# The border of mixing stage and feed in a single-core encoder step: the sample's columns of T1 and T2, the weights of three products, T1's parts and the second product change place

## The chip, the cores and the metric

One core of a Trainium2 chip (trn2) runs the whole step as one program. The time is the device time of one execution in microseconds; lower is better. The engines are TensorE (PE), VectorE (DVE), ScalarE (ACT), GpSimd (POOL) and SyncE (SP), the last used here only to issue DMAs.

## The reference, cut to what matters

One layer of an encoder for 1024 prompt rows and 64 sample rows of width 1024, in float32. The change lies where the first of these lines ends and the feed begins; projection and attention ahead of them are not touched.

```python
hp = xp + mixed @ w_out                      # mixing stage, 1024 prompt rows
xp = hp + _swiglu(hp, norm_ffn_g, w_gate, w_up, w_down)   # the feed
hs = xs + mixed_s @ w_out                    # the same for 64 sample rows
xs = hs + _swiglu(hs, norm_ffn_g, w_gate, w_up, w_down)

def _swiglu(h, g, w_gate, w_up, w_down):
    n = _rms_norm(h, g)
    return (silu(n @ w_gate) * (n @ w_up)) @ w_down
```

## The kernel before, in words

**Numbers in two parts.** Every matrix product is made of three: each float32 operand is split into a high part (a cast to the engine's reduced form, by ACT) and a low part (operand minus high part, by DVE or POOL), and PE adds high*high, high*low and low*high.

**The feed's products.** `n @ w_gate` and `n @ w_up` are made with seven products instead of eight (a Strassen-Winograd scheme): n, transposed, has four blocks B11, B21, B12, B22 (`raw_n[0][0]`, `raw_n[1][0]`, `raw_n[0][1]`, `raw_n[1][1]`), each 128 partitions by 4 groups by 544 rows of n. The first index is the half of the 1024 features, the second the half of the 1088 rows. The sample's 64 rows are the last 64 columns (480 to 543) of B12 and B22. Four sums are needed: T1 = B12 - B11 (written over B11), T2 = B22 - T1 (in `spare`), T3 = B22 - B12 (over B12), T4 = B21 - T2 (over B21). Product 0 takes B11, 1 B21, 2 T2, 3 T1, 4 T3, 5 T4, 6 B22. The parts of operand k lie in `part_hi[k]` and `part_lo[k]`. A product of a unit u is 24 matmuls: two column halves of 272, four feature groups, three part pairs (L2799 to L2801 in `feed`, L2056 to L2058 where it is made in the mixing stage). There are 22 units (11 pairs of 128 columns of each of gate and up).

**The weights' side.** Of each 256 columns of a weight the blocks a11, a12, a21, a22 and four sums (`s1`, `s2`, one in place, `s4`; `w_sum_dve`, L2579) are the stationary operands. ACT casts each one's high part into a ring of six slots (L2036, L2466), POOL writes the low part (L2042, L2430). Slot 0 of the first unit lies in an unused corner of `mT_hi`, slots 1 and 2 in `shared` where w_out's low half lay (free once the last mixing product is done).

**The mixing stage** (`mix`) goes through nine row tiles, in the order 0, 4, 1, 5, 2, 6, 3, 7 and last the sample's (index 8, 64 rows). Per tile: PE multiplies by w_out (two halves), DVE adds the residual (L1872, L1870), ACT takes the squares (L1833), POOL the root (L66, L68), DVE the norm (`xn`, L1877), PE turns `xn` (`turn_n`, L1967), ACT copies the result into `raw_n` (L1843). After each pair of tiles 128 more columns of all four blocks are there ("chunk"; the first has 96, since the second half of the rows begins at row 544), and ACT and DVE make the parts of B11 and B21 (L1812, L1885), T1 and T2 (L1894, L1896), T2's parts (L1818, L1911), and T3 and T4 (L1904, L1905) of it. After the last chunk's B11 parts PE makes the first product at the stage's end (`first_product_pe`), ahead of the sample's `turn_n`.

**The border.** `mix` and `feed` are two blocks: no engine begins the second before all have ended the first. Within a block each engine has its own queue in program order, and semaphores say what it waits for: `n_hi` and `n_lo` count high and low parts of n, `sums` the T's, `w_sums`, `w_hi_done`, `w_lo_done` the weights', `multiplied` finished products.

**The feed's first unit.** DVE begins with T1, T2 of the sample's columns, T2's low part of them (L2544, L2548, L2563), T3 of them (L2552), all of T1's low part (544 columns times 4 = 2176 elements), one weight sum (L2579), T4 of them (L2556), then the sums of products 0 to 2 from PSUM (L2596, L2600), T3's low part (L2563), and so on. ACT begins with T2's high part, the weight of product 2, T1's high part (L2474) and the weight of product 3. PE begins with product 1, SP loads the next unit's weights once T4 is done (L2012).

## Time and profile before

| | us |
|---|---|
| median of 3 runs | 1459.32 (1458.92 to 1460.43) |
| the profiled execution, its own time | 1457.65 |
| its span, first to last instruction | 1455.9 |
| PE busy | 1390.5 (96%) |
| DVE busy | 1023.3 (70%) |
| ACT busy | 627.0 (43%) |
| POOL busy | 391.7 (27%) |
| mixing stage ends, feed begins (in the span) | about 748 |
| mean granted TensorE clock | 0.985 of full |

Times of rows are microseconds from the span's start. An engine's busy time is that of its instructions; a matmul counts until its modelled end, so two in a row overlap. The profile names the idle time before an instruction in square brackets with what ended it; "issue" is a wait for nothing that the profile shows, "PEq" is the sequencer of PE, which is how the border of two blocks appears.

### The profile page before, as it was taken

What the parts mean: (1) busy time and instruction counts of PE and PEld (TensorE: products, weight loads), DVE (VectorE), ACT (ScalarE), POOL (GpSimd) and SP (SyncE); (2) the same over time, 40 slices, a digit from 0 to 9 for tenths busy, and PEclk for the clock granted to TensorE, in tenths of its full rate; (3) what the DMA queues carried; (4) which work ended last, traced back from release to release, by engine and by line L of the source; (5) the groups of instructions that cost most, each with busy time, mean ns of one, the idle gap of its engine ahead of it and who ended that gap; (6) DMA issues with size and microseconds to landing.
All of it is one profiled execution on the core that took longest, in us unless ns stands there. A gap on an engine that the chain in (4) does not pass through costs nothing. (4 is left out here: it accounts for less than half of the span.)

```text
span 1455.9 us, 23782 instructions
## 1 busy us (share of the span) xinstructions
PE 1390.5 (96%) x9152; PEld 1197.5 (82%) x9152; DVE 1023.3 (70%) x1378; ACT 627.0 (43%) x1154; POOL 391.7 (27%) x319
## 2 busy tenths in 40 slices
PE   7999999789999999999979999999999999999998
PEld 5778888667777766678869999999999998788886
DVE  6886868598876878955688666676666667654466
ACT  7524333268887776623253232222223223543343
POOL 2100000100010000011136454455445445654344
PEclk9999999889999999999999999999999999999999
DMA  7232320364443555453313444443344447954454
GB/s 253 74 136 95 116 76 33 129 187 119 125 104 105 145 144 163 120 167 122 105 54 136 147 140 161 147 169 132 119 145 162 146 154 237 346 176 159 160 181 174
DMA packets 176936, 209.66 MB, mean 144 GB/s; under 512 B 19456, under 2 KB 118136, under 8 KB 175416
## 3 DMA queue, kind: packets, MB, share of 16 engines
q1 hardware_dynamic: 171992, 197.32, 42.0%
q10 hardware_dynamic: 4832, 10.82, 2.0%
q8 instruction: 74, 1.21, 0.3%
q14 instruction: 38, 0.31, 0.1%
HBM read 148.78 MB, written 59.31 MB: 143 GB/s over the span
## 5 line engine op out<-in xcount | busy, mean ns | idle before, releaser
L1613 PE MATMUL ps_aT<-ident,z 128*128 128x128 f32 (+1 forms) x568 | 96.5, 286 | 2.1 <-DVE z L1447 2.1
L1269 ACT COPY aT<-ps_aT 128x512 f32<-128x512 f32 (+2 forms) x168 | 86.6, 523 | 26.1 <-PE ps_aT L1613 25.4
L683 PE MATMUL ps_proj<-shared 128*128 128x512 f32 x224 | 90.1, 402 | 4.6 <-DVE shared L540 3.0
L685 PE MATMUL ps_proj<-shared 128*128 128x512 f32 x224 | 88.3, 394 | 0.0
L684 PE MATMUL ps_proj<-shared 128*128 128x512 f32 x224 | 88.3, 394 | 0.0
L2480 ACT COPY aux<-ps_feed 128x544 f32<-128x544 f32 x22 | 13.5, 612 | 170.1 <-PE ps_feed L2801 170.1
L2430 POOL TENSOR_TENSOR ring_more<-staging,ring_more 128x512 fp32r<-128x512 f32 x45 | 69.4, 1547 | 56.5 <-ACT ring_more L2466 56.4
L1613 PEld LDWEIGHTS ps_aT<-ident,z 128*128 128x128 f32 (+1 forms) x568 | 63.8, 142 | 24.8 <-issue 14.7
L2430 POOL TENSOR_TENSOR shared<-staging,shared 128x512 fp32r<-128x512 f32 x41 | 60.0, 1468 | 86.0 <-ACT shared L2466 86.0
L1447 DVE TENSOR_TENSOR_SCAN z<-z,near 128x1024 f32<-128x1024 f32 (+7 forms) x64 | 82.7, 1337 | 0.0
L2694 DVE TENSOR_TENSOR blocks<-ps_feed,blocks 128x512 f32<-128x512 f32 x56 | 35.9, 681 | 66.0 <-PE ps_feed L2830 66.0
L2799 PE MATMUL ps_feed<-shared,ring_more 128*128 128x272 f32 x264 | 76.6, 290 | 1.8 <-issue 1.8
L2799 PE MATMUL ps_feed<-parts_early,shared 128*128 128x272 f32 x256 | 74.5, 291 | 2.1 <-PEq L1691 2.1
L2801 PE MATMUL ps_feed<-shared,ring_more 128*128 128x272 f32 x264 | 76.2, 289 | 0.0
L2800 PE MATMUL ps_feed<-shared 128*128 128x272 f32 x264 | 76.1, 288 | 0.0
L2800 PE MATMUL ps_feed<-parts_early,ring_more 128*128 128x272 f32 x264 | 76.1, 288 | 0.0
L2801 PE MATMUL ps_feed<-shared 128*128 128x272 f32 x264 | 76.1, 288 | 0.0
L2800 PE MATMUL ps_feed<-shared,ring_more 128*128 128x272 f32 x264 | 76.1, 288 | 0.0
L2801 PE MATMUL ps_feed<-parts_early,ring_more 128*128 128x272 f32 x264 | 76.0, 288 | 0.0
L2799 PE MATMUL ps_feed<-parts_early,ring_more 128*128 128x272 f32 x264 | 76.0, 288 | 0.0
L2799 PE MATMUL ps_feed<-shared 128*128 128x272 f32 x264 | 75.6, 286 | 0.0
L2800 PE MATMUL ps_feed<-parts_early,shared 128*128 128x272 f32 x256 | 74.5, 291 | 0.0
(351 smaller groups left out, 4520.4 us busy)
## 6 DMA issues: line engine op xcount, KB each, us to landing
staging<-s_dram SPq DMA_DIRECT2D x50, 256.0 KB, 3.6
staging<-in_w_gate SPq DMA_DIRECT2D x11, 1024.0 KB, 7.8
blocks<-in_w_up SPq DMA_DIRECT2D x11, 1024.0 KB, 5.4
blocks<-in_w_down SPq DMA_DIRECT2D x11, 1024.0 KB, 9.8
t_dram<-blocks SPq DMA_DIRECT2D x11, 1024.0 KB, 3.9
s_dram<-blocks SPq DMA_DIRECT2D x11, 1024.0 KB, 5.2
w_raw<-in_w_in SPq DMA_DIRECT2D x10, 1024.0 KB, 5.3
staging<-t_dram SPq DMA_DIRECT2D x30, 256.0 KB, 4.1
```

Source lines behind the costliest of these rows:

```text
L683: nc.tensor.matmul(res, a_hi[:, k, cols], b_hi[:, k], start=start, stop=False)
L684: nc.tensor.matmul(res, a_hi[:, k, cols], b_lo[:, k], start=False, stop=False)
L685: return nc.tensor.matmul(res, a_lo[:, k, cols], b_hi[:, k], start=False, stop=(k == HK - 1))
L1269: last = nc.scalar.copy(aT[:, G % AT, 0:f], ps_aT[:, G % 2, 0:f])
L1447: nc.vector.tensor_tensor_scan(back, back, mask[:, ::-1], 1.0, ALU.mult, ALU.max).then_inc(ready, 1)
L1613: last = nc.tensor.transpose(ps_aT[0:m, G % 2, k], z(x, at, m), t["ident"][:, :])
L2430: nc.gpsimd.tensor_tensor(w_lo, product_source(m)[0], w_hi.bitcast(F32), ALU.subtract).then_inc(w_lo_done, 1)
L2480: nc.scalar.copy(two(first), bank(u, 0)).then_inc(first_done, 1)
L2694: nc.vector.tensor_tensor(place, ps, place, ALU.add).then_inc(corners[name], 1)
L2799: nc.tensor.matmul(res, w_hi[:, k], x_hi, start=(k == 0), stop=False)
L2800: nc.tensor.matmul(res, w_hi[:, k], x_lo, start=False, stop=False)
L2801: last = nc.tensor.matmul(res, w_lo[:, k], x_hi, start=False, stop=(k == HK - 1))
```

## The change

- **Mixing stage, PE:** `first_product_pe` takes the number of the product. Product 0 is made where it was; after the sample's `turn_n` product 1 follows, out of the feed.
- **Weights:** ACT casts the blocks of products 1 and 2 after the last mixing product (before: 1), POOL corrects both ahead of the sample's `row_norm` (before: 1 after it); both leave the feed.
- **T1 and T2 of the sample's columns** and T2's parts of them are made at the end of the mixing stage, as a fifth chunk (480 to 543).
- **T1's parts:** columns 0 to 479 in the mixing stage (ACT ahead of the sample's copies, DVE after T2's low part of the fourth chunk), 480 to 543 as the feed's first work.
- **T3 and T4 of the fourth chunk** (352 to 479) leave the mixing stage and are made in the feed together with the sample's columns (192 columns times 4 = 768 elements each), ahead of the weight sum.
- The counts that waits ask for are shifted accordingly. No DMA is added or removed.

```diff
@@ -1747,6 +1747,13 @@
         NC = len(chunks)
+        chunks.append((ends[-1], TH))
+        def t2_made(c):
+            return 4 * c + 2 if c < NC else 4 * NC
         block = ctx.enter_context(nc.Block())
@@ -1786,10 +1793,13 @@
             for i in range(NT + 1):
+                if i == NT:
+                    w_low_pool(nc, pool, t, 1)
+                    w_low_pool(nc, pool, t, 2)
                 if i >= 1:
                     row_norm(i - 1)
-                if i >= NT - 1:
-                    w_low_pool(nc, pool, t, i - NT + 1)
+                if i == NT - 1:
+                    w_low_pool(nc, pool, t, 0)
                 if i + 2 < NT:
@@ -1814,7 +1824,7 @@
                 a, b = chunks[c]
-                act.wait_ge(sums, 4 * c + 2)
+                act.wait_ge(sums, t2_made(c))
                 nc.scalar.copy(part_hi[2][:, :, a:b], t["spare"][:, :, a:b]).then_inc(n_hi, 1)
@@ -1825,6 +1835,7 @@
                     w_high_act(nc, act, t, 1)
+                    w_high_act(nc, act, t, 2)
                 if i >= 1:
@@ -1837,6 +1848,10 @@
                         w_high_act(nc, act, t, 0)
+                    if i == NT:
+                        high_sum(NC - 1)
+                        nc.scalar.copy(part_hi[3][:, :, 0:ends[-1]], raw_n[0][0][:, :, 0:ends[-1]]).then_inc(n_hi, 1)
                     for j in range(2):
@@ -1844,8 +1859,9 @@
                     high_first(i // 2 - 1)
-                if i >= 3 and i % 2 == 1:
+                if i >= 3 and i % 2 == 1 and i < NT:
                     high_sum(i // 2 - 1)
+            high_sum(NC)
@@ -1889,25 +1905,25 @@
                 b11, b12, b22 = raw_n[0][0][:, :, a:b], raw_n[0][1][:, :, a:b], raw_n[1][1][:, :, a:b]
-                dve.wait_ge(n_out, 4 * (c + 1))
-                dve.wait_ge(n_lo, 3 * c + 1)
+                dve.wait_ge(n_out, min(4 * (c + 1), 2 * NT))
+                dve.wait_ge(n_lo, 3 * min(c, NC - 1) + 1)
                 nc.vector.tensor_tensor(b11, b12, b11, ALU.subtract).then_inc(sums, 1)
-                dve.wait_ge(sums, 4 * c + 1)
+                dve.wait_ge(sums, t2_made(c) - 1)
                 nc.vector.tensor_tensor(t["spare"][:, :, a:b], b22, b11, ALU.subtract).then_inc(sums, 1)
 ...
                 b12, b21, b22 = raw_n[0][1][:, :, a:b], raw_n[1][0][:, :, a:b], raw_n[1][1][:, :, a:b]
-                dve.wait_ge(sums, 4 * c + 2)
-                dve.wait_ge(n_lo, 3 * c + 2)
+                dve.wait_ge(sums, t2_made(c))
+                dve.wait_ge(n_lo, 3 * min(c, NC - 1) + 2)
                 nc.vector.tensor_tensor(b12, b22, b12, ALU.subtract).then_inc(sums, 1)
 ...
                 a, b = chunks[c]
-                dve.wait_ge(n_hi, 3 * c + 3)
+                dve.wait_ge(n_hi, 3 * c + 3 if c < NC else 3 * NC + 2)
                 nc.vector.tensor_tensor(part_lo[2][:, :, a:b], t["spare"][:, :, a:b],
@@ -1941,8 +1957,12 @@
                     w_sum_dve(nc, dve, t, 1)
-            second_sums(NC - 1)
             low_sum(NC - 1)
+            dve.wait_ge(n_hi, 3 * NC + 1)
+            nc.vector.tensor_tensor(part_lo[3][:, :, 0:ends[-1]], raw_n[0][0][:, :, 0:ends[-1]],
+                                    part_hi[3][:, :, 0:ends[-1]].bitcast(F32), ALU.subtract).then_inc(n_lo, 1)
+            first_sums(NC)
+            low_sum(NC)
@@ -2000,8 +2020,11 @@
             pe.wait_ge(m_lo, 2 * NT)
-            first_product_pe(nc, pe, t, 3 * NC - 2)
+            first_product_pe(nc, pe, t, 0, 3 * NC - 2)
             turn_n(NT - 1)
+            pe.wait_ge(h_added, 2 * (NT - 1))
+            first_product_pe(nc, pe, t, 1, 3 * NC - 1)
@@ -2017,6 +2040,10 @@
     return x[:, 0:HK, 0:P], x[:, HK:, 0:P], x[:, 0:HK, P:], x[:, HK:, P:]
+def first_factor(t, m):
+    return t["s2"] if m == 2 else first_blocks(t)[m]
@@ -2033,26 +2060,28 @@
     act.wait_ge(t["pair_loaded"][0], 16)
-    nc.scalar.copy(t["ring_first"][m][0], first_blocks(t)[m]).then_inc(t["w_hi_done"], 1)
+    if m == 2:
+        act.wait_ge(t["w_sums"], 2)
+    nc.scalar.copy(t["ring_first"][m][0], first_factor(t, m)).then_inc(t["w_hi_done"], 1)
 ...
     w_hi, w_lo = t["ring_first"][m]
-    nc.gpsimd.tensor_tensor(w_lo, first_blocks(t)[m], w_hi.bitcast(F32), ALU.subtract).then_inc(t["w_lo_done"], 1)
-def first_product_pe(nc, pe, t, parts_done):
-    pe.wait_ge(t["w_lo_done"], 1)
+    nc.gpsimd.tensor_tensor(w_lo, first_factor(t, m), w_hi.bitcast(F32), ALU.subtract).then_inc(t["w_lo_done"], 1)
+def first_product_pe(nc, pe, t, m, parts_done):
+    pe.wait_ge(t["w_lo_done"], m + 1)
     pe.wait_ge(t["n_lo"], parts_done)
-    w_hi, w_lo = t["ring_first"][0]
+    w_hi, w_lo = t["ring_first"][m]
     HK, CW = w_hi.shape[1], t["half"] // 2
 ...
         cols = slice(c * CW, (c + 1) * CW)
-        res = t["ps"][:, 0, c, 0:CW]
+        res = t["ps"][:, m, c, 0:CW]
         for k in range(HK):
-            x_hi, x_lo = t["part_hi"][0][:, k, cols], t["part_lo"][0][:, k, cols]
+            x_hi, x_lo = t["part_hi"][m][:, k, cols], t["part_lo"][m][:, k, cols]
             nc.tensor.matmul(res, w_hi[:, k], x_hi, start=(k == 0), stop=False)
@@ -2286,11 +2315,7 @@
-            return 3 * (NT // 2) + max(0, k - 1)
-        def sums_done(k):
-            return 4 * (NT // 2) + k
+            return 3 * (NT // 2) + 2 + max(0, k - 2)
@@ -2298,7 +2323,7 @@
                     sp.wait_ge(n_lo, parts_done(2))
-                    sp.wait_ge(sums, sums_done(4))
+                    sp.wait_ge(sums, 4 * (NT // 2) + 2)
                 elif u >= 2:
@@ -2424,7 +2449,7 @@
         def _(pool):
-            for m in range(2, M):
+            for m in range(3, M):
                 pool.wait_ge(w_hi_done, m + 1)
@@ -2467,10 +2492,10 @@
-                src = (spare, raw_n[0][0], raw_n[0][1], raw_n[1][0], raw_n[1][1])[k - 2]
-                cols = slice(near if k == 2 else 0, TH)
-                if k < 6:
-                    act.wait_ge(sums, sums_done((2, 1, 3, 4)[k - 2]))
+                src = (raw_n[0][0], raw_n[0][1], raw_n[1][0], raw_n[1][1])[k - 3]
+                cols = slice(near if k == 3 else 0, TH)
+                if k in (4, 5):
+                    act.wait_ge(sums, 4 * (NT // 2) + k - 3)
                 nc.scalar.copy(part_hi[k][:, :, cols], src[:, :, cols]).then_inc(n_hi, 1)
@@ -2509,8 +2534,6 @@
-            split_n(2)
-            split_w(2)
             split_n(3)
@@ -2535,31 +2558,19 @@
         def _(dve):
-            def sum_n(k):
-                rest = slice(near, TH)
-                b11, b12, b21, b22 = raw_n[0][0], raw_n[0][1], raw_n[1][0], raw_n[1][1]
-                if k == 0:
-                    dve.wait_ge(n_lo, parts_done(1))
-                    nc.vector.tensor_tensor(b11[:, :, rest], b12[:, :, rest], b11[:, :, rest],
-                                            ALU.subtract).then_inc(sums, 1)
-                elif k == 1:
-                    dve.wait_ge(sums, sums_done(1))
-                    nc.vector.tensor_tensor(spare[:, :, rest], b22[:, :, rest], b11[:, :, rest],
-                                            ALU.subtract).then_inc(sums, 1)
-                elif k == 2:
-                    dve.wait_ge(sums, sums_done(1))
-                    nc.vector.tensor_tensor(b12[:, :, rest], b22[:, :, rest], b12[:, :, rest],
-                                            ALU.subtract).then_inc(sums, 1)
-                else:
-                    dve.wait_ge(sums, sums_done(2))
-                    nc.vector.tensor_tensor(b21[:, :, rest], b21[:, :, rest], spare[:, :, rest],
-                                            ALU.subtract).then_inc(sums, 1)
+            def sum_n():
+                rest = slice(near - P, TH)
+                b12, b21, b22 = (x[:, :, rest] for x in (raw_n[0][1], raw_n[1][0], raw_n[1][1]))
+                dve.wait_ge(sums, 4 * (NT // 2))
+                dve.wait_ge(n_lo, parts_done(2))
+                nc.vector.tensor_tensor(b12, b22, b12, ALU.subtract).then_inc(sums, 1)
+                nc.vector.tensor_tensor(b21, b21, spare[:, :, rest], ALU.subtract).then_inc(sums, 1)
             def split_n(k):
-                src = (spare, raw_n[0][0], raw_n[0][1], raw_n[1][0], raw_n[1][1])[k - 2]
-                cols = slice(near if k == 2 else 0, TH)
+                src = (raw_n[0][0], raw_n[0][1], raw_n[1][0], raw_n[1][1])[k - 3]
                 dve.wait_ge(n_hi, parts_done(k))
+                cols = slice(near if k == 3 else 0, TH)
                 nc.vector.tensor_tensor(part_lo[k][:, :, cols], src[:, :, cols], part_hi[k][:, :, cols].bitcast(F32),
@@ -2712,13 +2723,9 @@
-            sum_n(0)
-            sum_n(1)
-            split_n(2)
-            sum_n(2)
             split_n(3)
+            sum_n()
             sum_w(0, 2)
-            sum_n(3)
             for u in range(NU):
@@ -2847,7 +2854,7 @@
             for u in range(NU):
-                for s in range(0 if u else 1, NPROD):
+                for s in range(0 if u else 2, NPROD):
                     product(u, s)
@@ -2962,9 +2969,9 @@
-            at = 6 * WIDTH + 2 * HK * P
-            t["ring_first"] = [None, [shared[:, at + a * HK * P:at + (a + 1) * HK * P]
-                                      .rearrange("p (k n) -> p k n", k=HK) for a in range(2)]]
+            at = 6 * WIDTH
+            t["ring_first"] = [None] + [[shared[:, at + (2 * m + a) * HK * P:at + (2 * m + a + 1) * HK * P]
+                                         .rearrange("p (k n) -> p k n", k=HK) for a in range(2)] for m in (1, 2)]
             mix(nc, t)
```

## Rows read from the trace of the kernel before

**Rows 1.** Windows by stage: length, busy us of PE, PEld, DVE, ACT, POOL (instructions), clock, DMA.
```profile
741.00:756.50 15.50, 9.03 (x58) 8.67 (x57) 11.59 (x15) 8.35 (x12) 6.30 (x5) 0.78 0.08 18
756.50:776.00 19.50, 16.30 (x126) 15.73 (x125) 18.45 (x16) 7.80 (x10) 14.00 (x7) 1.00 0.50 162
776.00:1206.00 430.00, 430.00 (x3432) 430.00 (x3431) 283.25 (x314) 119.57 (x182) 210.24 (x146) 1.00 0.42 145
```

**Rows 2.** Timeline of PE, 738 to 770: start, us, line, out<-in [idle before <-releaser].
```profile
738.02 0.29 PE L2056 MATMUL ps_feed<-parts_early,mT_hi 128*128 128x272 f32 x1
...
740.91 0.29 PE L2058 MATMUL ps_feed<-parts_early,mT_hi 128*128 128x272 f32 x1
...
745.55 0.78 PE L1967 MATMUL ps_feed<-ident,xn 64*128 64x64 f32 x8 [4.35 <-DVE xn L1877]
...
748.45 0.56 PE L2799 MATMUL ps_feed<-parts_early,shared 128*128 128x272 f32 x1 [2.12 <-PEq L1691]
...
752.67 0.38 PE L2799 MATMUL ps_feed<-parts_early,shared 128*128 128x272 f32 x1
...
760.67 0.36 PE L2799 MATMUL ps_feed<-shared,ring_more 128*128 128x272 f32 x1 [0.96 <-issue]
...
769.40 0.36 PE L2799 MATMUL ps_feed<-part_late,shared 128*128 128x272 f32 x1 [1.45 <-issue]
```

**Rows 3.** Timeline of DVE, 718 to 761.
```profile
718.37 1.28 DVE L1877 SCALAR_TENSOR_TENSOR xn<-h_ring,rstd,g 128x1024 f32<-128x1024 f32 x1 [1.47 <-POOL rstd L68]
...
736.40 1.82 DVE L1885 TENSOR_TENSOR parts_early<-blocks,parts_early 128x768 fp32r<-128x768 f32 x2
...
741.74 0.69 DVE L1896 TENSOR_TENSOR blocks<-blocks 128x512 f32<-128x512 f32 x1
...
743.22 2.28 DVE L1877 SCALAR_TENSOR_TENSOR xn<-h_ring,rstd,g 64x1024 f32<-64x1024 f32 x1 [0.79 <-POOL rstd L68]
...
747.29 0.69 DVE L1911 TENSOR_TENSOR parts_early<-blocks,parts_early 128x512 fp32r<-128x512 f32 x1 [0.59 <-ACT parts_early L1818]
...
748.30 0.42 DVE L2544 TENSOR_TENSOR blocks<-blocks 128x256 f32<-128x256 f32 x1 [0.32 <-PEq L1691]
...
749.66 0.43 DVE L2563 TENSOR_TENSOR parts_early<-blocks,parts_early 128x256 fp32r<-128x256 f32 x1 [0.47 <-ACT parts_early L2474]
...
752.09 2.43 DVE L2563 TENSOR_TENSOR shared<-blocks,shared 128x2176 fp32r<-128x2176 f32 x1 [1.67 <-ACT shared L2474]
...
754.43 1.78 DVE L2579 TENSOR_TENSOR staging<-staging 128x512 f32<-128x512 f32 x1
...
757.73 2.85 DVE L2563 TENSOR_TENSOR shared<-blocks,shared 128x2176 fp32r<-128x2176 f32 x1
```

**Rows 4.** Timeline of ACT, 738 to 752.
```profile
738.22 0.62 ACT L2036 CAST shared<-staging 128x512 fp32r<-128x512 f32 x1 [1.45 <-PE ps_feed L1990]
...
746.05 0.69 ACT L1843 COPY blocks<-ps_feed 128x256 f32<-128x256 f32 x2 [3.76 <-PE ps_feed L1967]
...
749.22 0.40 ACT L2474 CAST parts_early<-blocks 128x256 fp32r<-128x256 f32 x1 [1.97 <-DVE blocks L2548]
...
750.05 2.00 ACT L2474 CAST shared<-blocks 128x2176 fp32r<-128x2176 f32 x1
```

**Rows 5.** Timeline of POOL, 743 to 756.
```profile
743.16 1.26 POOL L2042 TENSOR_TENSOR shared<-staging,shared 128x512 fp32r<-128x512 f32 x1
...
752.65 3.01 POOL L2430 TENSOR_TENSOR ring_more<-staging,ring_more 128x512 fp32r<-128x512 f32 x1 [1.08 <-ACT ring_more L2466]
```

**Rows 6.** Windows round the slow stretch, columns as in rows 1.
```profile
741.00:746.00 5.00, 0.65 (x9) 0.45 (x8) 4.18 (x5) 1.15 (x2) 1.96 (x3) 1.00 0.24 52
746.00:747.00 1.00, 0.33 (x5) 0.14 (x2) 0.70 (x2) 0.95 (x3) 0.00 (x0) 0.53 0.00 0
752.00:753.00 1.00, 1.00 (x6) 1.00 (x6) 0.91 (x1) 1.00 (x4) 0.35 (x1) 0.56 0.06 16
```

**Rows 7.** Timeline of SP's queue, the feed's first load.
```profile
756.62 0.38 SPq L2012 DMA_DIRECT2D blocks<-in_w_up  x1
```

## The prediction, made before any run of the change

> **What bounds the kernel now.** I read the windows by stage first. From 776 to 1206 us TensorE (PE) is busy for all of its 430 us, so whatever time is won or lost ahead of 776 simply moves that stretch. Between 741.0 and 776.0, round the border of mixing stage and feed, it is busy 25.3 of 35 us [rows 1]: the only gap that the change touches. The rest of the argument is about which wait ends last there.
>
> The PE timeline names the gaps [rows 2]. The first product's 24 matmuls begin at 738.02 and 740.91 (0.126 us apart) and end at 741.20; PE then waits 4.35 us for the sample's normalized rows, turns them (745.55 to 746.33), and waits 2.12 us for the end of the mixing block. The second product starts at 748.45; until 752.67 its matmuls stand some 0.23 us apart. Products are numbered from 0 in the code, and I call them P0 to P6. P4 starts at 760.67 and P6 at 769.40, each after an idle stretch marked "issue".
>
> The DVE timeline says what these wait for [rows 3]. P4's last need is the low part of T3, which DVE ends at 760.58, 0.09 us ahead. The slow matmuls of P1 and P2 cost nothing by themselves: P3 was done 0.96 us before P4 could start. **So P4's start is set by DVE's queue from the block's first instruction (748.30): 12.37 us.** I call the block's start F; before, F = 748.30. P4 to P6 follow at the distances that DVE and POOL give them (8.73 us from P4 to P6).
>
> **POOL and DVE exclude each other.** POOL's correction of 512 columns takes 1.26 us at 743.16, but 3.01 us at 752.65, where DVE's 2176-column subtraction is under way; DVE's next 512-column sum then takes 1.78 instead of 0.69, and its norm at 743.22 takes 2.28 beside POOL against 1.28 at 718.37 [rows 3, 5]. In each pair the later one ends about its undisturbed time after the earlier one. I use that as a rule for SBUF-only operations.
>
> **The change in the mixing stage.**
> *Weights.* ACT casts two blocks after P0 of the last tile's mixing instead of one: 738.22 plus two times 0.62, done near 739.4; its next work, the sample's squares, waits for DVE's last addition, which ends where T1 of the last chunk begins, near 741.0, so this costs nothing. POOL's two corrections go ahead of the sample's statistics: 738.9 to 741.5, and the statistics come after that, ending just ahead of 743.22. The corrections hold DVE's T1 sum, due near 741.0, by about 0.3, so T2 ends at 742.7 rather than 742.43 [rows 3 to 5]. No DMA is added.
> *The norm.* With POOL's correction gone from 743.16, the norm takes 1.28: it ends at 744.55 instead of 745.50, and the sample's transposes run 744.6 to 745.4. PE's wait falls from 4.35 to 3.4 us.
> *ACT* has T2's high part (0.62, 742.75 to 743.4) and then T1's high part of 480 columns times 4 = 1920: between 0.40 for 256 and 2.00 for 2176 [rows 4] that is 1.8, so until 745.1. The sample's two copies queue behind it and end at 745.8; their transposes end at 745.4, so little waits.
> *DVE* has T2's low part (0.69, in the shade of ACT's), then T1's low part: between 0.69 for 512 and 2.43 for 2176, 2.16 for 1920, from 745.2 to 747.3. T1 and T2 of the sample's columns, ACT's high and DVE's low part follow. Before, the same four steps took from 748.30 to 750.09, 1.8 us [rows 3, 4]. DVE ends at 749.05, 1.07 later than the 747.98 of before.
> *PE.* P1 follows the transposes at 745.4: its weights (741.5) and part (before 741) are there. At full clock its 24 matmuls end at 748.5, under DVE's 749.05. At 1.2 GHz throughout they take 5.45 and end at 750.9.
>
> **The clock is the unknown.** PE is granted 1.00 until 746, 0.53 in 746 to 747, and 0.56 in 752 to 753 [rows 6], the last slow spacing being at 752.67, that is, it fell near 746.06 after 4.35 us of idleness and 0.8 us of small transposes, and rose 4.4 us after matmuls resumed. Now it idles 3.4 us and then works on. Bounds: no fall, P1 ends at 748.5; fall at 746.06 and rise 4.4 us after 745.4, five matmuls fast, some 16 slow, the rest fast: 750.15; an earlier rise ends it at 749.6. I take the half-slow case, as the row of before is nearest: PE ends at about 749.9 and becomes the last to reach the block's end. The Trainium skill (TensorE: Matmul & The Clock Gate, Part 1) calls the activity monitor free-running, so that the number of slow matmuls differs between runs of one kernel; by that the fast and the half-slow case would both occur here, and one profile shows only one of them.
> From the last instruction (747.98) to DVE's first in the feed lie 0.32 us. **F becomes 750.2 (749.35 if the clock stays).**
>
> **The change in the feed, from F.** Gone: T1 and T2 of 64 columns, T2's parts of them, and T1's parts of 480 columns. What is left ahead of P4 on DVE: T1's last low part after ACT's 0.40, until 0.87; T3 and T4 of 192 columns, 768 elements, 0.91 each [rows 3]. POOL's correction for P3 is ready near 1.0, gets in after T3 (1.7) and ends at 2.9; T4 runs behind it to 3.7. The weight sum, 0.69: 4.4. Two sums from PSUM, which between 756.21 and 757.73 took 1.2 beside a short one: 5.6. POOL's correction for P4 was ready at about 5.05 and holds the lock to 6.35; T3's low part, 2.43, ends at 8.65. **P4 starts at F + 8.7 instead of F + 12.37.** P2 (F + 0.15, 3.0 us) and P3 (needs POOL at 2.9) end by F + 6.3, or by F + 8.1 if half of them is slow: still under the cover of DVE's chain. SP's load of the next pair waits for T4 (F + 3.7, about 754 rather than 756.62 [rows 7]), so P7 has its weights sooner than before; nothing else waits in that queue. P5 and P6 keep their distances.
>
> **Sum.** P4 at 750.2 + 8.7 = 758.9, against 760.67: 1.8 us saved (1.07 of DVE's work and some 0.8 of PE's lateness are added ahead of F, 3.67 taken behind it). All later work moves with it. The profiled run has a span of 1455.9 and a time of 1457.65, 1.7 below the median of 1459.32; taken off the median: **1457.5 us**. Changes of about 0.2% (2.9 us) are what a measurement tells from none, so this is likely to read as no change.
>
> The Trainium skill (SBUF — State Buffer, SBUF: two separate sides) states the lock as held for a whole instruction, by any GpSimd operation that reads SBUF. Were that so for the one-column statistics too, which before ran in the 0.79 us that DVE was idle ahead of 743.22 [rows 3], T2's sum, now ending at 742.7 and not at 742.43, would hold them by 0.3 us, and P1 would start and, in the half-slow case, end 0.3 later: 1457.8. No row of before shows that pair with such an overlap.
>
> **Rivals.**
> *The clock never falls.* For: only 3.4 us idle, and a 1.45 us wait before 769.40 left it at 1.00 [rows 1, 2]. Then DVE sets F at 749.35, P4 starts at 758.05, 2.6 us saved: 1456.7.
> *The exclusion turns out kinder.* If DVE gets T4 in ahead of POOL's first correction, or T3's low part ahead of its second, the chain ahead of P4 shortens by 0.7 (a DVE operation of 2.43 instead of waiting 0.7 first): with the clock up, 3.3 saved, 1456.0. Against: POOL is ready 0.4 us before DVE in the second pair.
> *The clock stays down.* P1 wholly at 1.2 GHz holds the mixing block until 750.95: F = 751.3, P4 at 760.0, 0.7 saved (1458.6). PE then idles from about F + 6.3 to F + 8.7, 2.4 us instead of 0.96; should the clock fall on that, P4 takes 5.4 instead of 3.0. The idle stretches ahead of P5 and P6 (8.73 us for two products of 3.2) cover part of the 2.4 us; the sums that DVE makes of P4 do not get that cover, so I put the price between 0 and 2.4, at 1.5: 0.8 lost in all, 1460.1. It decides for slower once P1 ends after 751.6. Against: the clock rose 4.4 us after work resumed.
> *Nothing left of it*: P4 waits for something else (weights of P3, T3's high part behind ACT's other casts). ACT's T3 part needs T3 at 1.75 and ends near F + 3.9, so there are 2.3 us of room; this I fold into the case before.
>
> **How the numbers follow.** Half-slow clock 0.47 (1457.2 to 1457.9), clock never falls 0.28 (1456.4 to 1457.0), kinder exclusion 0.10, clock down or a new wait 0.15, a third of it past zero. The three runs of the kernel before spread over 1.5 us, so about 0.7 goes on either end: 1455.4 to 1459.5. Faster by over 0.2% needs 2.9 saved: the kinder case, a third of the no-fall case and a little of the rest, 0.26. Slower by over 0.2%: 0.05. Same: 0.69.
>
> **What would show it.** PE waits 3.4 us before the sample's transposes, norm at 1.3 us; P1's 24 matmuls between 745.4 and the block's end, with the granted clock telling which case it is; DVE's last mixing work near 749; feed starting near 750.2; P4 8.7 us later, ended by T3's low part; PE without a gap after P6. The prediction is wrong if P4 starts before 757.5 or after 760.2, if P1 runs after the block's border, or if a new idle stretch of PE appears past 776.

## The result and the profile after

The changed kernel takes 1461.43 us in the median of 13 runs, 1.0018 of the kernel before (95% interval 1.0010 to 1.0027), where 1457.5 was forecast within 1455.4 to 1459.5. Measured again in another set of 11 runs (e2 below) it took 1460.35 us, 1.0007 of before (0.9998 to 1.0016). So by the two sets the change costs 1.0 to 2.6 us (0.0007 and 0.0018 of 1459) instead of saving 1.8; the second set alone does not tell it from no change.

**How to compare.** The profiled execution of the change has a span of 1465.7 us, 9.8 above the one of before, but 5.5 of that lie ahead of anything the change touches. I therefore count from T, the start of the transposes of row tile 7, the last prompt tile (the expectations call it the seventh), shortly ahead of the border and shared by all kernels (733.41 before, 738.94 after). T itself lay anywhere from 731.7 to 738.9 in 13 profiles of kernels with the same code up to there. TensorE's timeline of the changed kernel, counterpart of [rows 2] (the transposes at T, the sample's, the first and the last matmul of product 1, the feed's first, product 4, product 6):

```profile
738.94 1.09 PE L1987 MATMUL ps_feed<-ident,xn 128*128 128x128 f32 x8 [1.53 <-DVE xn L1893]
...
750.33 1.12 PE L1987 MATMUL ps_feed<-ident,xn 64*128 64x64 f32 x8 [3.57 <-DVE xn L1893]
...
751.37 0.59 PE L2085 MATMUL ps_feed<-parts_early,shared 128*128 128x272 f32 x1
...
756.22 0.29 PE L2087 MATMUL ps_feed<-parts_early,shared 128*128 128x272 f32 x1
...
756.99 0.36 PE L2806 MATMUL ps_feed<-parts_early,shared 128*128 128x272 f32 x1 [0.48 <-PEq L1691]
...
765.60 0.41 PE L2806 MATMUL ps_feed<-shared,ring_more 128*128 128x272 f32 x1 [2.37 <-DVE shared L2574]
...
775.56 0.36 PE L2806 MATMUL ps_feed<-part_late,shared 128*128 128x272 f32 x1 [2.18 <-issue]
```

Read as times after T:

| after T, us | sample's transposes | feed's first product | P4 | P6 | P6 to the end | T to the end |
|---|---|---|---|---|---|---|
| before | 12.14 | 15.04 | 27.26 | 35.99 | 686.5 | 722.5 |
| forecast | 11.2 | 16.9 | 25.5 | 34.2 | 686.5 | 720.7 |
| after | 11.39 | 18.05 | 26.66 | 36.62 | 690.1 | 726.8 |
| after, second profile (e2) | 11.37 | 18.01 | 26.62 | 36.58 | 688.2 | 724.7 |

Product 4 came 0.6 us earlier than before instead of 1.8; then P4 to P6 took 9.96 us instead of 8.73, and what follows P6 got longer as well, by 1.7 us in the second profile and by some 2 more in the first, where the clock fell once again at 1257.3 us. The first profile is of the slowest of its 13 runs (1467.55 us), the second of a run near its median (1460.21). The windows say why (length, busy us of PE, PEld, DVE, ACT, POOL, granted clock, DMA): the clock fell while PE waited for the sample's rows, so that the transposes took 1.12 us instead of 0.78 and product 1 ran mostly at 1.2 GHz (0.67 in 747 to 752, 0.56 in 752 to 756; 17 of its 23 steps from matmul to matmul took over 0.2 us, most of them 0.23, where a fast one takes 0.126), and the clock fell twice more, at product 4 (0.72 in 764 to 768) and at product 6 (0.57 in 776 to 780). Before, everything from 756.5 to 1206 was at 1.00 [rows 1].

```profile
747.00:752.00 5.00, 1.67 (x11) 1.56 (x12) 4.26 (x5) 3.88 (x6) 0.98 (x3) 0.67 0.25 56
752.00:756.00 4.00, 4.00 (x21) 4.00 (x21) 2.13 (x4) 0.41 (x1) 0.00 (x0) 0.56 0.00 0
764.00:768.00 4.00, 2.40 (x11) 2.43 (x12) 4.00 (x3) 2.91 (x4) 2.33 (x2) 0.72 0.33 110
776.00:780.00 4.00, 4.00 (x22) 4.00 (x21) 3.36 (x5) 1.14 (x2) 2.37 (x2) 0.57 0.78 266
```

On DVE nearly everything went as in the sum. T1's sum is held by POOL (1.00 us), the norm takes 1.28 instead of 2.28 (but begins 0.2 later than forecast), T1's low part of 480 columns 2.15; the mixing work ends at 754.63, T + 15.69, forecast T + 15.64. Then DVE waits 2.62 us for the block's end, which product 1 holds up. From ACT's first instruction of the feed (756.81) to product 4 are 8.79 us, forecast 8.7.

```profile
746.57 1.00 DVE L1910 TENSOR_TENSOR blocks<-blocks 128x512 f32<-128x512 f32 x1
...
749.00 1.28 DVE L1893 SCALAR_TENSOR_TENSOR xn<-h_ring,rstd,g 64x1024 f32<-64x1024 f32 x1 [0.70 <-POOL rstd L68]
...
750.80 2.15 DVE L1962 TENSOR_TENSOR shared<-blocks,shared 128x1920 fp32r<-128x1920 f32 x1
...
754.21 0.42 DVE L1927 TENSOR_TENSOR parts_early<-blocks,parts_early 128x256 fp32r<-128x256 f32 x1 [0.47 <-ACT parts_early L1828]
...
757.25 0.43 DVE L2574 TENSOR_TENSOR shared<-blocks,shared 128x256 fp32r<-128x256 f32 x1 [2.62 <-ACT shared L2499]
...
770.42 0.72 DVE L2616 TENSOR_TENSOR blocks<-ps_feed,blocks 128x544 f32<-128x544 f32 x1 [0.90 <-PE ps_feed L2808]
```

The last row shows the next loss: DVE waits 0.90 us for the slow product 4 before it can add it, and the low part that product 6 needs stands behind those sums.

### The profile page after: what moved, and what is told of

Read it like the earlier page. It is cut to its first block and busy times, and to the rows that moved or that the text cites. A ratio compares the mean times of both kernels' runs of the same rounds, so it can differ in the third digit from the quotient of the medians.

```text
span 1465.7 us, 23783 instructions
## 1 busy us (share of the span) xinstructions
PE 1402.3 (96%) x9152; PEld 1207.0 (82%) x9152; DVE 1022.9 (70%) x1377; ACT 627.7 (43%) x1155; POOL 388.6 (27%) x319
## 5 line engine op out<-in xcount | busy, mean ns | idle before, releaser
L2806 PE MATMUL ps_feed<-parts_early,shared 128*128 128x272 f32 x248 | 71.2, 287 | 0.5 <-PEq L1691 0.5
L2807 PE MATMUL ps_feed<-parts_early,shared 128*128 128x272 f32 x248 | 71.4, 288 | 0.0
```

The source lines that it names most:

```text
L2806: nc.tensor.matmul(res, w_hi[:, k], x_hi, start=(k == 0), stop=False)
L2807: nc.tensor.matmul(res, w_hi[:, k], x_lo, start=False, stop=False)
```

## The experiments

Every kernel below was run up to 12 times, with the kernel before beside it on the same chip. "Theory C" is that the change saves what was forecast in work, and that the clock's falls at TensorE's waits take it back. All of them, with T and the times after T from the one profile of each:

| kernel | median us | ratio to before | T | feed | P4 | P6 | T to the end |
|---|---|---|---|---|---|---|---|
| e1 before again | 1459.59 | 1.0000 | 736.23 | 15.00 | 27.24 | 35.97 | 722.7 |
| e2 after again | 1460.35 | 1.0007 | 733.67 | 18.01 | 26.62 | 36.58 | 724.7 |
| e3 product 1 first | 1455.83 | 0.9976 | 731.73 | 16.15 | 25.13 | 33.85 | 722.3 |
| e4 the same, waits filled | 1454.69 | 0.9966 | 732.01 | 16.15 | 25.54 | 33.43 | 720.0 |
| e5 after, feed's waits filled | 1457.97 | 0.9997 | 736.02 | 17.28 | 25.85 | 34.57 | 721.3 |
| e6 product 1 in the feed | 1458.91 | 1.0001 | 735.12 | 16.16 | 27.17 | 34.89 | 722.0 |
| e7 before, border filled | 1458.91 | 0.9999 | 734.28 | 15.28 | 27.50 | 36.21 | 722.5 |
| e8 after, first wait filled | 1456.65 | 0.9984 | 735.96 | 16.16 | 24.77 | 34.73 | 722.4 |
| e9 as e4, filled longer | 1455.28 | 0.9975 | 733.71 | 16.19 | 24.76 | 33.48 | 719.5 |
| e10 as e9, feed not filled | 1455.16 | 0.9970 | 733.20 | 16.19 | 24.81 | 33.54 | 720.1 |
| e11 POOL's order as before | 1462.52 | 1.0020 | 735.11 | 19.45 | 28.05 | 36.76 | 723.6 |

**e1: the kernel before, unchanged.**

> The kernel before, unchanged, to see how its time and its clock falls spread. Theory C (the clock's falls in waits of 2 to 4 us decide, and where they land differs from run to run, in attention as well as at the border): its runs stay within 1457.5 to 1460.5, but a second profile shows falls at places other than the first one's (73.6, 281.8, 305.7, 435.4, 572.0, 626.6 and 746.1 us from the span's start). Rival F (falls are fixed by the program): the same places within 0.1 us.

Median 1459.59 against 1458.76 (ratio 1.000, 0.999 to 1.001), runs from 1456.9 to 1461.6, a little wider than expected. In its profile the falls came at 76.6, 284.8, 308.7, 438.4, 574.9, 629.5 and 749.0 us: the same waits, each about 3 us later, and the second and the fifth lasted longer. T is 736.23, 2.8 later than in the first profile, and the border is the same to 0.04 us:

```profile
736.23 1.09 PE L1967 MATMUL ps_feed<-ident,xn 128*128 128x128 f32 x8 [1.53 <-DVE xn L1877]
...
748.38 0.71 PE L1967 MATMUL ps_feed<-ident,xn 64*128 64x64 f32 x8 [4.35 <-DVE xn L1877]
...
763.47 0.37 PE L2799 MATMUL ps_feed<-shared,ring_more 128*128 128x272 f32 x1 [0.91 <-issue]
```

The falls are not tied to the program. The matmul behind the first wait that has one starts 0.97 us later here than in the first profile of before, and the fall comes 3.0 us later, in that profile 0.6 us ahead of this matmul and here 1.4 us behind it (first line before, second line e1):

```profile
74.18 0.79 PE L683 MATMUL ps_proj<-shared 128*128 128x512 f32 x1 [2.71 <-DVE shared L540]
75.15 0.50 PE L683 MATMUL ps_proj<-shared 128*128 128x512 f32 x1 [2.73 <-DVE shared L540]
```

Matmul for matmul e1 is 1.0 us behind the first profile ahead of that fall, 1.3 behind it, 3.0 at 310 us, 4.7 at 600 and 2.8 at T: most of what moves T comes in round the falls. The border of the kernel before came out the same in both profiles all the same, which is what allows the comparison from T.

**e2: the changed kernel, unchanged.**

> The changed kernel, unchanged. Theory C: times again spread over more than 5 us, their mean clock explains them (about 1.2 us for 0.001 of clock), and a profile with a clock near 0.983 shows the border from the transposes of the seventh tile's rows to product 6 at 34.0 to 35.5 us, against 35.99 before and 36.62 in the first profile of the change. Rival F: median 1461.4 within 1 us, border 36.6 us again.

Median 1460.35, runs from 1459.0 to 1463.1 (4.2 us, not more than 5). P6 comes at T + 36.58, as the rival said, not between 34.0 and 35.5 (the profile's clock is 0.981; the median is 1.1 us below the rival's 1461.4): with T 5.3 us earlier than in the first profile of the change, the border is the same to 0.04 us. Product 1 is slow in 18 of its 23 steps, products 4 and 6 in some 15 of theirs:

```profile
745.00:750.00 5.00, 4.96 (x25) 4.84 (x26) 3.84 (x5) 1.50 (x4) 0.00 (x0) 0.50 0.02 3
760.00:764.00 4.00, 3.71 (x17) 3.74 (x18) 4.00 (x3) 2.53 (x4) 2.68 (x2) 0.57 0.15 39
770.00:774.00 4.00, 3.75 (x18) 3.78 (x19) 3.90 (x6) 1.14 (x2) 1.67 (x2) 0.59 0.66 213
```

**e3: product 1 ahead of the sample's transposes.**

```diff
             first_product_pe(nc, pe, t, 0, 3 * NC - 2)
-            turn_n(NT - 1)
-
             pe.wait_ge(h_added, 2 * (NT - 1))
             first_product_pe(nc, pe, t, 1, 3 * NC - 1)
+            turn_n(NT - 1)
```

> Product 1 ahead of the sample's transposes, in the wait for their rows; nothing else differs from the change. Theory C: product 1 runs at 2.4 GHz (3.0 us), no longer ends the mixing block, which DVE then ends; the feed begins 1.9 us earlier than in the first profile of the change (16.2 us after the transposes of the seventh tile instead of 18.05), product 4 at 24.9 us instead of 26.66; 1457 to 1459 us in all. Rival B (the border's cost comes from DVE and POOL, not from product 1): product 4 stays at 26.5 us or later.

1455.83 us, 0.9976 of before (0.9966 to 0.9986), better than expected: this small exchange beats both kernels. Feed at T + 16.15, P4 at T + 25.13, P6 at T + 33.85, 2.1 us ahead of before.

```profile
742.24 0.28 PE L2086 MATMUL ps_feed<-parts_early,shared 128*128 128x272 f32 x1
...
743.10 0.71 PE L1987 MATMUL ps_feed<-ident,xn 64*128 64x64 f32 x8 [0.58 <-DVE xn L1893]
...
747.88 0.57 PE L2805 MATMUL ps_feed<-parts_early,shared 128*128 128x272 f32 x1 [4.07 <-PEq L1691]
...
756.86 0.36 PE L2805 MATMUL ps_feed<-shared,ring_more 128*128 128x272 f32 x1
...
765.58 0.37 PE L2805 MATMUL ps_feed<-part_late,shared 128*128 128x272 f32 x1 [1.44 <-issue]
```

PE's wait for the sample's rows shrinks to 0.58 us because product 1 lies in it, at full speed (its last recorded matmul starts at 742.24). The long wait is now the 4.07 us ahead of the feed, where the clock falls, but products 2 and 3 have room: P4 is set by DVE, whose low part of T3 ends at 756.76 though it had to wait 1.06 us for the slow product 2, and as the products fill the time up to it, PE does not wait ahead of P4 either. In this profile T is early and the stretch from T to the end only 0.2 to 0.4 us shorter than before, since the clock fell once more at 1245.5 us; the border itself is 2.1 shorter. Rival B is out.

**e4: e3 with unread matmuls in the waits.**

```diff
             turn_n(NT - 1)
+            fill_pe(nc, t, 2, 14)
...
+                if u == 0 and s in (4, 5, 6):
+                    fill_pe(nc, t, s - 4, {4: 14, 5: 4, 6: 8}[s])
                 if u == 0:
                     pe.wait_ge(n_lo, parts_done(s))
```

(`fill_pe` multiplies a part of B21 by itself into a free bank, `count` times; the next real product clears it.)

> As e3, with matmuls that nothing reads added where PE would wait: 14 after the sample's transposes, 14, 4 and 8 ahead of products 4, 5 and 6. Theory C: no fall of the clock after the transposes and none at products 4 to 6; product 6 at 33.6 us after the seventh tile's transposes, 8.7 after product 4; 1455.5 to 1457.5 us. Rival B: no gain over e3, since DVE sets products 4 to 6 anyway.

1454.69 us, 0.9966 of before (0.9953 to 0.9978); P6 at T + 33.43. The first expectation was missed: the 14 matmuls did not reach to the block's end, a wait of 2.11 us was left, and the clock fell 0.9 us into product 2. With P3 therefore later, the 14 matmuls ahead of P4 held it up: P4 at T + 25.54, not 24.9. Over e3 no gain is shown: P6 is 0.4 us earlier, but the two intervals overlap (five runs here), so rival B stands for this step.

**e5: the change, unread matmuls ahead of products 4, 5 and 6 only** (the second part of e4's edit, on the changed kernel).

> The change with matmuls that nothing reads ahead of products 4, 5 and 6 only (14, 4, 8); product 1 stays behind the sample's transposes. All counts from the transposes of the seventh tile's rows (T). Theory C: product 1 is wholly slow again and the feed begins at T + 17.7; product 4 at T + 26.6; but no fall at products 4 and 6, so product 6 at T + 35.3 (36.6 in the change) and no slow matmuls in it: 2.5 to 3 us under the change, 1457.5 to 1458.5 in all. Rival B: product 6 stays at T + 36.6.

1457.97 us, 0.9997 of before (0.9989 to 1.0006), P6 at T + 34.57 and 686.7 us behind it, like the kernel before. In this profile the clock was still up during the sample's transposes (0.71 us) and 14 of product 1's steps took 0.23 us, close to the case that the prediction took as likeliest: feed at T + 17.28, P4 at T + 25.85. The waits ahead of P4 to P6 are filled and the clock stays up there:

```profile
753.30 0.36 PE L2815 MATMUL ps_feed<-parts_early,shared 128*128 128x272 f32 x1 [0.48 <-PEq L1691]
...
759.39 1.92 PE L2094 MATMUL ps_feed<-parts_early 128*128 128x272 f32 x14
...
761.87 0.39 PE L2815 MATMUL ps_feed<-shared,ring_more 128*128 128x272 f32 x1 [0.56 <-DVE shared L2581]
...
770.59 0.39 PE L2815 MATMUL ps_feed<-part_late,shared 128*128 128x272 f32 x1 [0.41 <-DVE part_late L2581]
```

```profile
747.00:752.00 5.00, 4.62 (x28) 4.55 (x29) 4.18 (x6) 1.75 (x4) 0.00 (x0) 0.68 0.01 3
760.00:766.00 6.00, 5.20 (x40) 4.76 (x38) 6.00 (x4) 4.16 (x6) 4.01 (x2) 1.00 0.45 134
```

**e6: the change with product 1 back in the feed.**

```diff
             first_product_pe(nc, pe, t, 0, 3 * NC - 2)
             turn_n(NT - 1)
-            pe.wait_ge(h_added, 2 * (NT - 1))
-            first_product_pe(nc, pe, t, 1, 3 * NC - 1)
...
-                for s in range(0 if u else 2, NPROD):
+                for s in range(0 if u else 1, NPROD):
```

> The change with product 1 back in the feed; the rest of it (weights, T1, T2 and their parts in the mixing stage) stays. The mixing block ends by DVE at T + 15.7, the feed begins at T + 16.0. Theory C: products 1 to 3 then follow one another, the first part of them slow, some 11.3 us as before, so that product 4 is set by PE at T + 27.4 without a wait and product 6 at T + 36.1: no better than before, 1458.5 to 1459.5. Rival B (DVE sets product 4 whatever PE does): product 4 at T + 24.8.

1458.91 us, 1.0001 of before (0.9990 to 1.0011). The feed begins at T + 16.16, products 1 to 3 fill 11.0 us, and P4 starts at T + 27.17 behind a wait of 0.21 us only. Moving DVE's work out of the feed alone thus gains nothing at P4: with a slow clock three products of PE cover it. The path still runs over DVE: its sums wait 0.69 and 2.29 us for products 1 and 2, and T3's low part, behind these sums, ends 0.09 us ahead of P4. P6 came at T + 34.89, earlier than expected, since here DVE's weight sum ahead of P5 got in before POOL (0.68 us instead of 1.76); that is 1.1 us ahead of before, of which the median shows nothing.

```profile
751.28 0.57 PE L2803 MATMUL ps_feed<-parts_early,shared 128*128 128x272 f32 x1 [4.07 <-PEq L1691]
...
762.29 0.36 PE L2803 MATMUL ps_feed<-shared,ring_more 128*128 128x272 f32 x1 [0.21 <-issue]
...
770.01 0.36 PE L2803 MATMUL ps_feed<-part_late,shared 128*128 128x272 f32 x1 [1.46 <-issue]
```

```profile
759.10 0.72 DVE L2608 TENSOR_TENSOR blocks<-ps_feed,aux 128x544 f32<-128x544 f32 x1 [2.29 <-PE ps_feed L2805]
```

**e7: the kernel before, with PE kept at work at the border.**

```diff
             first_product_pe(nc, pe, t, 3 * NC - 2)
+            pe.wait_ge(h_added, 2 * (NT - 1))
+            pe.wait_ge(t["n_lo"], 3 * NC - 1)
+            fill_pe(nc, t, 1, 26)
             turn_n(NT - 1)
+            fill_pe(nc, t, 2, 14)
```

> The kernel before with 26 matmuls that nothing reads ahead of the sample's transposes and 14 behind them. The prediction said that the slow stretch at the border cost the kernel before nothing, since DVE set product 4: then product 4 stays at T + 27.2 with the clock up, and the time within 0.5 us of before. If the slow stretch did cost something, product 4 comes earlier than T + 26.8.

1458.91 us, 0.9999 of before (0.9990 to 1.0007). The clock stays up, product 3 can start earlier and is then held by POOL (0.82 us) and P4 by DVE (1.62 us instead of 0.96); P4 at T + 27.50, later by the 0.24 us by which the unread matmuls put off the feed (T + 15.28). The slow stretch cost the kernel before nothing.

```profile
741.91 3.41 PE L2069 MATMUL ps_feed<-parts_early 128*128 128x272 f32 x26
...
747.09 2.02 PE L2069 MATMUL ps_feed<-parts_early 128*128 128x272 f32 x14
...
756.90 0.36 PE L2810 MATMUL ps_feed<-shared,ring_more 128*128 128x272 f32 x1 [0.82 <-POOL ring_more L2441]
...
761.78 0.36 PE L2810 MATMUL ps_feed<-shared,ring_more 128*128 128x272 f32 x1 [1.62 <-issue]
```

**e8: the change in its own order, with the wait filled.**

```diff
             first_product_pe(nc, pe, t, 0, 3 * NC - 2)
+            pe.wait_ge(h_added, 2 * (NT - 1))
+            pe.wait_ge(t["n_lo"], 3 * NC - 1)
+            fill_pe(nc, t, 1, 24)
             turn_n(NT - 1)
-
-            pe.wait_ge(h_added, 2 * (NT - 1))
             first_product_pe(nc, pe, t, 1, 3 * NC - 1)
```

> The change in its own order, with 24 matmuls that nothing reads in the wait ahead of the sample's transposes. Theory C (the clock alone makes product 1 late, not its place): product 1 at 2.4 GHz ends by T + 15.0, DVE ends the mixing block at T + 15.7, product 4 at T + 24.8; what follows as in the change where a wait of 2.4 us is left (product 6 between T + 33.5 and T + 34.8): 1455.5 to 1457.5. Rival (the place matters): as the change, 1460 to 1461.5.

1456.65 us, 0.9984 of before (0.9976 to 0.9993). Nothing but 24 unread matmuls was added to the change (and two waits that are over by then), and the feed begins at T + 16.16 instead of 18.05, P4 at T + 24.77 instead of 26.66: 1.9 us. The clock, not the place of product 1, made it late. At P4 and P6 the clock still falls to 1.2 GHz (0.57 and 0.60), and P6 is at T + 34.73. This profile is of the slowest of the twelve runs (1460.23 us); the median lies 3.7 us under e2's, more than the 1.9 at P4, so in most runs less is probably lost behind P4 than here, which no profile shows:

```profile
743.59 3.17 PE L2095 MATMUL ps_feed<-parts_early 128*128 128x272 f32 x24
...
752.12 0.36 PE L2814 MATMUL ps_feed<-parts_early,shared 128*128 128x272 f32 x1 [0.87 <-PEq L1691]
...
760.73 0.56 PE L2814 MATMUL ps_feed<-shared,ring_more 128*128 128x272 f32 x1 [2.35 <-DVE shared L2582]
...
770.69 0.47 PE L2814 MATMUL ps_feed<-part_late,shared 128*128 128x272 f32 x1 [2.26 <-issue]
```

```profile
747.00:752.00 5.00, 3.91 (x32) 3.62 (x32) 4.14 (x6) 1.76 (x5) 0.00 (x0) 1.00 0.01 3
760.00:764.00 4.00, 3.27 (x14) 3.30 (x15) 4.00 (x3) 2.91 (x4) 2.67 (x2) 0.57 0.18 47
770.00:774.00 4.00, 3.31 (x15) 3.34 (x16) 3.90 (x6) 1.14 (x2) 1.24 (x1) 0.60 0.51 169
```

**e9: e4 with 26 unread matmuls behind the transposes instead of 14.**

> As e4 (product 1 first, 14, 4 and 8 unread matmuls ahead of products 4, 5, 6), but 26 unread matmuls behind the sample's transposes instead of 14, so that PE works until DVE ends the mixing block. Theory C: the clock does not fall at the border, products 2 and 3 run at 2.4 GHz, the 14 matmuls ahead of product 4 no longer hold it up: product 4 at T + 24.8 (25.54 in e4), product 6 at T + 33.4 or up to 0.7 earlier; 1454 to 1455. Rival: DVE and POOL alone set products 4 to 6 and nothing changes against e4.

1455.28 us, 0.9975 of before (0.9966 to 0.9984). No fall at the border; P4 at T + 24.76 and P6 at T + 33.48, as expected. Against e4 nothing is gained at P6: P4 is 0.78 us earlier and P6 follows it at 8.72 us instead of 7.89, as DVE's low parts, and not the start of P4, set P6.

**e10: e9 without the unread matmuls in the feed.**

> As e9 without the unread matmuls in the feed. PE then waits 2.4 us ahead of product 4, as it does in the change. Theory C: the clock falls on that wait as in e2 and e8, product 4 at T + 24.8 but slow, product 6 at T + 34.7 and itself slow: 1456 to 1457.5. Rival (a wait of 2.4 us is harmless if the border was fast): product 6 at T + 33.5.

1455.16 us, 0.9970 of before (0.9958 to 0.9981), six runs within 1.0 us. Here theory C's expectation failed: PE waits 2.37 us ahead of P4, as in the change, and the clock stays at 1.00. P6 comes at T + 33.54. The median, too, is that of e9, where these waits are filled.

```profile
745.25 3.53 PE L2096 MATMUL ps_feed<-parts_early 128*128 128x272 f32 x26
...
749.39 0.36 PE L2814 MATMUL ps_feed<-parts_early,shared 128*128 128x272 f32 x1 [0.61 <-PEq L1691]
...
758.01 0.36 PE L2814 MATMUL ps_feed<-shared,ring_more 128*128 128x272 f32 x1 [2.37 <-DVE shared L2582]
...
766.74 0.36 PE L2814 MATMUL ps_feed<-part_late,shared 128*128 128x272 f32 x1 [1.45 <-issue]
```

```profile
758.00:762.00 4.00, 3.25 (x24) 3.03 (x24) 4.00 (x3) 2.25 (x4) 2.68 (x2) 1.00 0.24 61
```

**e11: the change with POOL's corrections behind the statistics again.**

```diff
-                if i == NT:
-                    w_low_pool(nc, pool, t, 1)
-                    w_low_pool(nc, pool, t, 2)
                 if i >= 1:
                     row_norm(i - 1)
+                if i == NT:
+                    w_low_pool(nc, pool, t, 1)
+                    w_low_pool(nc, pool, t, 2)
```

> The change with POOL's two weight corrections behind the sample's statistics again. The norm of the sample's rows runs beside POOL: 2.28 us instead of 1.28, the sample's transposes at T + 12.1 instead of 11.4, product 1 behind a correction that ends near T + 11; the feed begins 0.8 later than in the change wherever product 1 is slow, product 6 at T + 37.3: 1461 to 1462. Rival (the order of POOL's work is worth nothing): as the change.

1462.52 us, 1.0020 of before (1.0009 to 1.0032). The norm takes 3.51 us, not 2.28, because there are now two corrections for it to wait out; the sample's transposes come at T + 13.37, the feed at T + 19.45, P6 at T + 36.76 (this profile has no fall at P4). The feed starts 1.4 us later than in the change. So the new order of POOL's work gains 1.4 us at the feed's start; at P6 (0.1 us) and in the medians (1.0020 against 1.0018 and 1.0007, with overlapping intervals) no gain of it is shown.

```profile
744.92 3.51 DVE L1893 SCALAR_TENSOR_TENSOR xn<-h_ring,rstd,g 64x1024 f32<-64x1024 f32 x1 [0.79 <-POOL rstd L68]
```

## Why the prediction was wrong

**What held.** The reading that a shift at the border carries over to the end where nothing behind P6 is slow (686.3 to 686.7 us from P6 to the end in before, e1, e4, e5, e7 and e10); the 8.7 us from the feed's start to P4 (8.79); the end of DVE's mixing work (T + 15.69 for 15.64); the norm at 1.28; the exclusion of DVE and POOL, by which T1's sum was to be held 0.3 (1.00 for 0.67 us); that the slow stretch was free before (e7). With the clock up, P4 comes at T + 24.77 (e8) where the no-fall rival had 758.05 - 733.41 = 24.64.

**The step that failed** is "The clock is the unknown" with what was built on it. It has three terms, here from the second profiles of both kernels (e2 against e1) where not said otherwise.

*Product 1's end.* "I take the half-slow case": PE ready near 749.9, T + 16.5. The number of slow steps was nearly right (some 16 forecast, 17 and 18 measured), the end was T + 17.57 in the first profile of the change. I had let the clock fall only after the transposes, as in the row of before; it fell in the wait ahead of them, so they ran slow too and product 1 began at T + 12.43 instead of 12.0; and it took 5.14 us to the end of its last matmul instead of 4.5. P4 came 0.62 us earlier than before, not 1.8. By e8, which adds nothing but work in that wait, the slow clock costs 1.89 us of P4's start; I had put in 0.85.

*P4 to P6.* I let the later products keep their distances. But PE's wait ahead of P4 grew from 0.9 to 2.33 us: products 2 and 3 alone fill 6.3 us of the feed where three products filled 11.3, while the time from the feed's first product to P4 only shrank from 12.2 to 8.6; the clock fell on it, the slow P4 held DVE's sums up by 0.90 us, and P6 came 9.96 instead of 8.73 us after P4: 1.23 lost.

*Product 6 and on.* The wait ahead of P6 grew with it from 1.44 to 2.17 us, the clock fell again, and 15 steps of product 6, each 0.1 us longer, had nothing left to hide behind: 1.45 lost (686.7 against 688.15 us).

Together 0.62 - 1.23 - 1.45 = -2.06, that is 2.06 us slower, or 1.0014 of before, which lies within the intervals of both sets. e5, which fills only the feed's waits, takes P4 to P6 back to 8.72 and the rest to 686.7, and so confirms the last two terms; e8 confirms the first.

The prediction's own signs would not have told. P4 at T + 26.66 is 760.07 on its scale, inside its 757.5 to 760.2, and none of them looked at the time from P4 to P6 or at product 6 itself.

**The rival "The clock stays down"** named this mechanism and two of its three places, product 1 and P4, at 1460.1 us; with "a new wait" it had a chance of 0.15. Its price left out product 6 itself. What should have raised its chance stood in my own sum: it forecast a wait of 2.4 us ahead of P4 where the trace of before showed the clock holding only up to 1.45.

**The two places that leaned on pages.** The Trainium skill (TensorE: Matmul & The Clock Gate, Part 1) calls the activity monitor free-running. The trace agrees: in e1 the first fall comes 3.0 us later than in the first profile, the matmul beside it only 0.97. I used that to mix a fast and a half-slow case; the slow cases were the ones that came.

The Trainium skill (SBUF — State Buffer, SBUF: two separate sides) gives the ports that DVE and GpSimd share to whichever starts first, for its whole instruction. The trace agrees, for one-column statistics too: beside T2's sum (which ends at 748.29) their first step takes 0.43 us in the changed kernel, and 0.18 in e11, where it starts as that sum ends. It is the 0.3 us that the prediction set beside its sum, and 0.2 of them arrived: the sample's transposes came at T + 11.39 instead of 11.2.

```profile
747.91 0.43 POOL L66 TENSOR_SCALAR ms<-sumsq 64x1 f32<-64x1 f32 x1 [0.90 <-ACT xn L1844]
```

```profile
744.07 0.18 POOL L66 TENSOR_SCALAR ms<-sumsq 64x1 f32<-64x1 f32 x1 [10.10 <-ACT xn L1844]
```

**Open.** Why one wait of 2.3 to 2.4 us lets the clock fall and another doesn't was not tried out. A candidate is chance, as at e1's first fall: falls came 0.1 us ahead of P4's start in e8, 0.2 behind it in the change and 0.9 behind the feed's start in e4, so that they aren't tied to the wait's end; but no run tests it. Open is also how much of the 1.1 us between the two medians of the change is where the falls ahead of T land.

## What to carry to other kernels

Taking one engine's work out of a stage that another engine bounds lengthens the first one's waits there; on TensorE a longer wait can cost more than itself, because the matmuls behind it run at half the clock. Put movable matmuls into an existing wait rather than behind it (e3: 2.9 us under before by the medians, by exchanging two calls of the change), and where none are left, unread ones do the same (e8, e10). Where the clock's falls move a kernel's stages by microseconds, compare profiles from the last common instruction, not by their spans.

## What was not expected of the hardware

Where the clock was up when a wait began, it fell at seven of nine waits of 2.1 to 2.4 us at or behind the border (P4 and P6 in the change, e2 and e8, the border in e4), and not at P4 in e10 and e11, with waits of 2.37 and 2.32 us; it never fell at the shorter waits there (P6 in before, e1, e3, e6, e7, e10 and e11 with 1.43 to 1.46, P4 in e7 with 1.62). The length of the wait alone does not decide it. The spread of the whole kernel's time goes with the clock too: in the 13 runs of the change the mean granted clock went from 0.986 (1454.6 us) to 0.975 (1467.6 us), nearly in the order of the times.
